# Sparse weights added float by float into a cleared DRAM array, and three blocks of tokens by rows instead of two

## The chip, the cores and the metric

One core of one Trainium2 chip runs the whole program. The metric is the device time in microseconds (us) of one execution. TensorE multiplies, VectorE (DVE), ScalarE (ACT) and GpSimd (POOL) work beside it, SyncE (SP) issues most DMAs, and all DMAs share 16 DMA engines.

## The reference, cut to what matters

One layer over 1024 tokens of width 1024: a mixing part (RG-LRU, SSD, a merge), which the change hardly touches, and then a layer of 16384 experts:

```
q = (x @ w_q)                       # 8 heads, two halves of 128
s = einsum(q, sub_keys)             # 128 scores per head and half
sv, si = top_k(s, 16)               # of each half
cv, ci = top_k(all 256 sums, 16)    # 16 experts per token and head
idx = i1 * 128 + i2;  g = softmax(cv)
act = gelu(sum_d expert_down[idx] * x)
y = sum over 8*16 experts of g * act * expert_up[idx]
```

Each token so uses 128 of the 16384 experts. Everything is float32; a product is made of three float32r products of the high and low parts.

## The kernel before, in words

The 1024 tokens are 8 blocks of 128. `NA = 2` blocks are computed **by rows**: for each of a token's 128 experts one indirect DMA of GpSimd fetches a row of `expert_down` for all 128 tokens (512 KB), and VectorE multiplies it with the tokens and sums (`dots`, L2002). The other 768 tokens (`TD`) are computed **dense**: TensorE multiplies all 128 tiles of 128 experts with them, and the result is later multiplied by a sparse array of weights that is zero for experts not chosen.

The stages that matter, each closed by a barrier of all engines:

- `project_in` (to about 850 us): 64 tiles of the input projection. SP loads a tile of weights, GpSimd cuts it into high and low part, TensorE multiplies.
- `queries` (1605 to 1872 us): 16 query tiles. TensorE makes queries (`query`, L1606, the first half as 256 + 256 columns, since the row tokens lie in a buffer of their own) and scores (`scores`, L1617). The scores of all blocks go to DRAM. VectorE chooses the experts of block 0, one head after each pair of tiles (`choose`: `select_keys`, then `select_picks`, whose end waits for an exponential of ScalarE).
- `experts_down` (1872 to 3384 us): 64 steps of two tiles of 128 experts. Per tile TensorE turns it (8 transposes, `turn`, L1864), ScalarE and VectorE cut it (`cut`, `low`, L1979), and TensorE makes 48 products of 128x384 (`products`, L1874); ScalarE applies the gelu and stores it in DRAM. Beside that each step chooses the experts of one head of one later block (56 of 64 steps), does four row products (`ROWS = 4` buffers), and from block 2 on builds the weights of 16 tokens: VectorE makes one-hot matrices (`hits`, L1988, L1992), TensorE multiplies them token by token (`weights`, L1885, 16 products a step), ScalarE copies them out (L1943), and SP stores them in DRAM as pieces of 64 tokens. `ps_d` and `downT` have one and two buffers.
- `experts_up` (3384 to 4649 us): 32 groups of four tiles. SP loads tile, gelu and weights (the weights in runs of 64 floats); VectorE multiplies the two; ScalarE, VectorE and GpSimd cut them (L2212, L2214, L2268, L2178); TensorE makes 12 slots of 12 products of 128x512 (`L2381`), which VectorE adds into `y_acc`. Beside that a group does two **quads** (L2340): four row fetches of GpSimd each (L2171), for four experts at once of 32 tokens each, and 8 products against `row_spread` (L2257). There is one set of row buffers.

The order of work on each engine is written out by hand; most of it stands in hardware loops (`Fori`) before. Every wait is on a semaphore, and each engine works in order, so what is written behind a waiting instruction waits too.

Of the kernel before, what the change touches and what calls it, by code (L numbers as in the profile page):

```python
# [40 lines left out]
NEG = -30000.0  # L41

# [315 lines left out]
def project_in(m, inp, keep, scratch):  # L358
# [10 lines left out]
    with ExitStack() as st:  # L369
# [6 lines left out]
        dt_bias = m.sb(st, "dt_bias", [P, SH])  # L376
        pre = m.sb(st, "conv_in", [P, 2, CW - 1 + T])
# [8 lines left out]
        s_abs, s_e, s_u, s_c = (m.sb(st, n, [P, NS]) for n in ("sp_abs", "sp_exp", "sp_one_plus", "sp_corr"))  # L386
# [16 lines left out]
        h_stored = m.sem("lru_h_stored")  # L403

# [18 lines left out]
        with nc.Block() as block:  # L423
            @block.sync
            def _(sp):
# [18 lines left out]
                for lo, hi, col in SEGMENTS[1:]:  # L444
                    pairs(sp, lo, hi, load(col))

            @block.gpsimd
# [944 lines left out]
SEL_STEPS = 25  # L1392

SCORES_READ = 6

def selection(m, st, tag):
# [3 lines left out]
    for name, shape, dt in (("scores", [P, 2, PK], F32), ("scores_rest", [P, 2, PK], F32), ("top", [P, 2, TOPK], F32),  # L1402
# [3 lines left out]
                            ("ij_f", [P, 2, TOPK], F32), ("neg_max", [P, 1], F32),  # L1406
                            ("exp", [P, TOPK], F32), ("exp_sum", [P, 1], F32), ("inv", [P, 1], F32)):
        b[name] = m.sb(st, f"{tag}_{name}", shape, dt)
    b["hit"] = m.sb(st, f"{tag}_hit", [P, 2, TOPK, TOPK])
# [3 lines left out]
def select_keys(dve, b, step, keep, n):  # L1413

    sc, rest, top, idx = b["scores"], b["scores_rest"], b["top"], b["idx"]

    def after(k):
        dve.wait_ge(step, (n + 1) * SEL_STEPS + k)

    after(0)
    alone(dve, keep["dve_passed"])
# [3 lines left out]
    alone(dve, keep["dve_passed"])  # L1426
# [4 lines left out]
    alone(dve, keep["dve_passed"])  # L1431
# [3 lines left out]
    alone(dve, keep["dve_passed"])  # L1435
# [6 lines left out]
def select_picks(dve, b, step, exp_done, keep, n, out):  # L1442
# [3 lines left out]
    iota, idx = keep["iota_row"], b["idx"]  # L1446

    def after(k):
        dve.wait_ge(step, (n + 1) * SEL_STEPS + k)
# [3 lines left out]
    alone(dve, keep["dve_passed"])  # L1453
# [3 lines left out]
    alone(dve, keep["dve_passed"])  # L1457
# [4 lines left out]
    alone(dve, keep["dve_passed"])  # L1462
    dve.max(b["cv"][:, 8:16], flat(b["cand_rest"])).then_inc(step, 1)
    after(17)
    alone(dve, keep["dve_passed"])
# [14 lines left out]
    dve.reduce_sum(out(slice(1, 3)), b["hit"][:], axis=AX.X).then_inc(step, 1)  # L1480
    dve.wait_ge(exp_done, n + 1)
# [994 lines left out]
```

## Time and profile before

| | us |
|---|---|
| three runs | 4647.34, 4653.0, 4651.68 (median 4651.68) |
| the profiled execution | 4650.75 |
| its span, first to last instruction | 4649.0 |
| PE busy in it | 4286.5 (92%) |
| DVE busy | 2599.5 (56%) |
| ACT busy | 1341.0 (29%) |
| POOL busy | 1432.2 (31%) |
| HBM read and written | 674.03 MB and 163.58 MB |

PE is TensorE's products, PEld its weight loads, which overlap them. Shares of busy time are means over the stages. Matmuls are pipelined: a row's duration is longer than the distance to the next one, and it is the distance that adds up to time.

### The profile page before, as it was taken

What the parts mean: (1) busy time and instruction counts of PE and PEld (TensorE: products, weight loads), DVE (VectorE), ACT (ScalarE), POOL (GpSimd) and SP (SyncE); (2) the same over time, 40 slices, a digit from 0 to 9 for tenths busy, and PEclk for the clock granted to TensorE, in tenths of its full rate; (3) what the DMA queues carried; (4) which work ended last, traced back from release to release, by engine and by line L of the source; (5) the groups of instructions that cost most, each with busy time, mean ns of one, the idle gap of its engine ahead of it and who ended that gap; (6) DMA issues with size and microseconds to landing.
All of it is one profiled execution on the core that took longest, in us unless ns stands there. A gap on an engine that the chain in (4) does not pass through costs nothing. (4 is left out here: it accounts for less than half of the span.)

```text
span 4649.0 us, 69126 instructions
## 1 busy us (share of the span) xinstructions
PE 4286.5 (92%) x22902; PEld 3639.0 (78%) x22933; DVE 2599.5 (56%) x5422; ACT 1341.0 (29%) x2021; POOL 1432.2 (31%) x1022
## 2 busy tenths in 40 slices
PE   8999999897997799799999999999979999999998
PEld 3788877686776689798999999999957777777776
DVE  3555211255665333677889898897644444444444
ACT  1132433344222421233333333333221111111112
POOL 0333333354334021222111111111144444444442
PEclk9999999899998899899999999999989999999999
DMA  7222233344562422555566665666587777777776
GB/s 272 56 95 95 99 104 98 93 118 118 165 195 90 152 64 63 177 198 197 173 215 218 204 207 198 219 215 210 199 270 245 248 246 249 246 250 248 251 248 213
DMA packets 632585, 838.99 MB, mean 180 GB/s; under 512 B 227732, under 2 KB 448164, under 8 KB 632484
## 3 DMA queue, kind: packets, MB, share of 16 engines
q1 hardware_dynamic: 514468, 476.96, 32.5%
q0 software_dynamic: 73728, 268.47, 17.3%
q10 hardware_dynamic: 44288, 92.29, 5.1%
q8 instruction: 54, 0.88, 0.1%
q14 instruction: 47, 0.39, 0.0%
HBM read 674.03 MB, written 163.58 MB: 180 GB/s over the span
## 5 line engine op out<-in xcount | busy, mean ns | idle before, releaser
L1874 PE MATMUL p_u<-h2T_hi,downT_hi 128*128 128x384 f32 x2048 | 715.0, 349 | 103.4 <-DVE downT_lo L1979 85.3
L1874 PE MATMUL p_u<-h2T_hi,downT_lo 128*128 128x384 f32 x2048 | 693.9, 339 | 0.0
L1874 PE MATMUL p_u<-h2T_lo,downT_hi 128*128 128x384 f32 x2048 | 692.8, 338 | 0.0
L1852 POOL DMA_INDIRECT down_rows<-in_peer_down_dram,row_ids x256 | 262.4, 1025 | 1264.4 <-DVE row_dots L2002 1187.8
L2381 PE MATMUL p_y<-up_hi,coef_hi 128*128 128x512 f32 x1488 | 587.2, 395 | 0.0
L2381 PE MATMUL p_y<-up_lo,coef_hi 128*128 128x512 f32 x1488 | 580.4, 390 | 0.0
L2381 PE MATMUL p_y<-up_hi,coef_lo 128*128 128x512 f32 x1488 | 579.4, 389 | 0.0
L2282 DVE TENSOR_TENSOR y_acc<-p_y,y_acc 128x512 f32<-128x512 f32 x372 | 256.4, 690 | 540.5 <-PE p_y L2381 540.5
L1874 PEld LDWEIGHTS p_u<-h2T_hi,downT_hi 128*128 128x128 f32 x2048 | 391.3, 191 | 116.4 <-issue 116.4
L2178 POOL TENSOR_TENSOR up_lo<-up_raw,up_hi 128x1024 fp32r<-128x1024 f32 x128 | 323.0, 2524 | 419.8 <-ACT up_hi L2212 418.7
L508 PE MATMUL p<-hT_hi,w_hi 128*128 128x512 f32 x1024 | 405.0, 396 | 0.0
L508 PE MATMUL p<-hT_hi,w_lo 128*128 128x512 f32 x1024 | 398.8, 389 | 0.0
L508 PE MATMUL p<-hT_lo,w_hi 128*128 128x512 f32 x1024 | 398.6, 389 | 0.0
L1874 PEld LDWEIGHTS p_u<-h2T_lo,downT_hi 128*128 128x128 f32 x2048 | 391.7, 191 | 0.0
L1874 PEld LDWEIGHTS p_u<-h2T_hi,downT_lo 128*128 128x128 f32 x2048 | 390.5, 191 | 0.0
L2381 PEld LDWEIGHTS p_y<-up_hi,coef_hi 128*128 128x128 f32 x1488 | 279.5, 188 | 111.3 <-issue 54.5
L2214 ACT CAST coef_hi<-gelu_in 128x768 fp32r<-128x768 f32 x128 | 106.8, 834 | 793.8 <-DVE gelu_in L2266 793.8
L2171 POOL DMA_INDIRECT up_rows<-in_peer_up_dram,row_ids_turned x256 | 263.4, 1029 | 226.3 <-PE p_rows L2340 161.8
L2381 PEld LDWEIGHTS p_y<-up_hi,coef_lo 128*128 128x128 f32 x1488 | 279.5, 188 | 59.4
L2381 PEld LDWEIGHTS p_y<-up_lo,coef_hi 128*128 128x128 f32 x1488 | 279.6, 188 | 56.2
L2002 DVE CUSTOM_DVE_ANT_0 row_products<-down_rows,x_tok_rows 128x1024 f32<-128x1024 f32 x256 | 311.8, 1218 | 12.1 <-DVE row_u L2010 6.4
L1931 ACT ACTIVATE gelu_out<-p_u 128x384 f32<-128x384 f32 x256 | 126.6, 495 | 595.3 <-PE p_u L1874 594.5
(343 smaller groups left out, 7888.8 us busy)
## 6 DMA issues: line engine op xcount, KB each, us to landing
down_raw<-in_peer_down_dram SPq DMA_DIRECT2D x128, 512.0 KB, 4.4
up_raw<-in_peer_up_dram SPq DMA_DIRECT2D x128, 512.0 KB, 5.3
scratch_gu<-gelu_out ACTq DMA_DIRECT2D x128, 384.0 KB, 2.3
gelu_in<-scratch_gu SPq DMA_DIRECT2D x128, 384.0 KB, 4.1
weights_in<-scratch_w SPq DMA_DIRECT2D x128, 384.0 KB, 6.4
w_raw<-in_w_in_dram SPq DMA_DIRECT2D x64, 512.0 KB, 4.0
w_ada_sb<-in_w_ada_dram SPq DMA_DIRECT2D x12, 2048.0 KB, 15.4
scratch_w<-weights_out SPq DMA_DIRECT2D x48, 512.0 KB, 3.7
```

The lines of the kernel that those rows point to most:

```text
L508: mm = pe.matmul(ps[u][:, half, :], w[:, u, k, :], hT[h][:, k, half * TH:(half + 1) * TH], start=(n == 0), stop=(n == 3 * KD - 1))
L1852: pool.indirect_dma_start(out=rows[:, n % ROWS, :], out_offset=None, in_=inp["peer_down"][0], in_offset=bass.IndirectOffsetOnAxis(ap=row_i ...
L1874: mm = pe.matmul(ps_u[u][half][:, 0:HD], d[:, u, k, :], h2[h][:, k, half * HD:(half + 1) * HD], start=(n == 0), stop=(n == 3 * KD - 1))
L1931: act.activation(gu[:, u, half * HD:(half + 1) * HD], ps_u[u][half][:, 0:HD], ACT.Gelu).then_inc(gelu_done[u][half], 1)
L2002: dve.tensor_tensor_reduce(junk[:], rows[:, j, :], x_tok[:, a], 1.0, 0.0, ALU.mult, ALU.add, dot[:, j:j + 1]).then_inc(dot_done, 1)
L2171: pool.indirect_dma_start(out=rows[:, j, :], out_offset=None, in_=inp["peer_up"][0], in_offset=bass.IndirectOffsetOnAxis(ap=ids_t[:, a, t: ...
L2178: pool.tensor_tensor(up_lo[:, g % 2, j, :], up_raw[:, u], up_hi[:, g % 2, j, :].bitcast(F32), ALU.subtract).then_inc(up_lo_done, 1)
L2214: act.copy(g_hi[:, v, j, :], gu[:, u]).then_inc(g_hi_done, 1)
L2282: dve.tensor_tensor(part, ps_y[s % BANKS][:], part, ALU.add).then_inc(added, 1)
L2381: mm = pe.matmul(ps_y[s % BANKS][:], a[:, v, j, t * P:(t + 1) * P], b[:, v, j, half * TH:(half + 1) * TH], start=(n == 0), stop=(n == 3 * ...
```

## The change

`NA` goes from 2 to 3: 384 tokens by rows, 640 dense (`TD = 640`, products of 320 columns, 10 slots instead of 12 in the up stage, three quads a group instead of two). The weights are no longer built with one-hot products. A DRAM array `w` of [128, 128, 640] floats is cleared in `project_in` by 64 stores of zeros, one behind each weight load on SP's queue. For each head of a dense block, 16 indirect DMAs of GpSimd, each of 128 single floats, one per token, add the weights into it (`send_weights`): 5 heads of block 3 in `queries`, 35 heads in `experts_down`. Before the first 16 of a head GpSimd waits for the previous head's 16 to have landed. In `queries` VectorE chooses 13 heads instead of 8.

```
-NA = 2
+NA = 3
@@ project_in, SP
                         sp.dma_start(w_raw[:, u], w_in(col, i)).then_inc(w_loaded[u], 16)
+                        if isinstance(i, int) and i == 0:
+                            sp.wait_ge(zero_set, 1)
+                        sp.dma_start(scratch["w"][bass.ds(i * CLEAR, CLEAR)].rearrange("e p t -> p e t"),
+                                     zero[:].unsqueeze(1).to_broadcast([P, CLEAR, TD])).then_inc(w_cleared, 16)
+                pool.memset(zero[:], 0.0).then_inc(zero_set, 1)
@@ new: the end of a head's choice, and the sending
+def select_end(dve, b, step, exp_done, n, id_f, ids, scale, weight, chosen):
+    dve.wait_ge(step, n * SEL_STEPS + 24)
+    dve.scalar_tensor_tensor(id_f, b["pick"][:, 0], float(PK), b["pick"][:, 1], ALU.mult, ALU.add).then_inc(step, 1)
+    dve.wait_ge(exp_done, n + 1)
+    dve.reciprocal(b["inv"][:], b["exp_sum"][:]).then_inc(step, 1)
+    dve.wait_ge(step, n * SEL_STEPS + 25)
+    if scale is None:
+        dve.tensor_copy(ids, id_f).then_inc(step, 1)
+    else:
+        dve.tensor_scalar(ids, id_f, float(TD), scale, ALU.mult, ALU.add).then_inc(step, 1)
+    dve.wait_ge(step, n * SEL_STEPS + 26)
+    dve.tensor_scalar(weight, b["exp"][:], b["inv"][:], None, ALU.mult).then_inc(chosen, 1)
+def send_weights(pool, b, w_flat, sent, chosen, k, part):
+    r, half = k % SENT, TOPK // 2
+    if part == 0:
+        pool.wait_ge(chosen, k + 1)
+        if k:
+            pool.wait_ge(sent[(k - 1) % SENT], 16 * TOPK * ((k - 1) // SENT + 1))
+    for j in range(part * half, part * half + half):
+        pool.indirect_dma_start(out=w_flat, out_offset=bass.IndirectOffsetOnAxis(ap=b["sent_ids"][:, r, j:j + 1], axis=0),
+                                in_=b["sent_g"][:, r, j:j + 1], in_offset=None, compute_op=ALU.add
+                                ).then_inc(sent[r], 16)
@@ queries, GpSimd, behind the cut of query tile n
+                    if n >= 5 and (n - 5) // 2 < EARLY:
+                        send_weights(pool, sel, w_flat, sent, weights_chosen, (n - 5) // 2, (n - 5) % 2)
@@ experts_down, order of heads: 16 pairs (dense, fetched), then 19 dense, over steps 0 to 59
+        fetched = [(a, h) for a in range(1, NA) for h in range(PH)]
+        dense = [(NA, h) for h in range(EARLY, PH)] + [(b, h) for b in range(NA + 1, TB) for h in range(PH)]
+        heads = [x for pair in zip(dense, fetched) for x in pair] + dense[len(fetched):]
@@ experts_down, GpSimd: 6 fetches a step (RING = 14 buffers), and the head of two steps before
+                for c in range(2 * FETCH):
+                    fetch(c)
+                for s in range(STEPS + 2):
+                    for c in range((s + 2) * FETCH, min((s + 3) * FETCH, TA)):
+                        fetch(c)
+                    if s >= 2 and head_of(s - 2) is not None and heads[head_of(s - 2)] in dense:
+                        for part in range(2):
+                            send_weights(pool, sel, w_flat, sent, weights_chosen, k, part)
+                        k += 1
@@ experts_down, VectorE: one step
+                    if 2 * s + 2 < E1:
+                        low(2 * s + 2)
+                    if before is not None:
+                        choose(before)
+                    for c in range(s * FETCH, s * FETCH + FETCH // 2):
+                        dot(c)
+                    if head is not None:
+                        dve.wait_ge(s_loaded[head % 2], 16 * (head // 2 + 1))
+                        select_keys(dve, sel, step, head)
+                    if 2 * s + 3 < E1:
+                        low(2 * s + 3)
+                    for c in range(s * FETCH + FETCH // 2, (s + 1) * FETCH):
+                        dot(c)
+                    if head is not None:
+                        select_picks(dve, sel, step, iota, head)
-                def hits(hh, r, ws, b):
-                def weights(ws, pair):
-                def keep_weights(hh, r, ws, b):
-                def store_piece(tile, hh, piece, stored=None):
@@ experts_up: two sets of row buffers, three quads a group
+    SETS = 2 if NA > 2 else 1
+    SPREADS = 2 * NA
+                        sp.dma_start(w[:, u], scratch["w"][n]).then_inc(w_loaded[u], 16)
+                        for q in range(NA):
+                            if s == (q + 1) * SLOTS // (NA + 1):
+                                quad(g * NA + q)
```

Further: `raw`, `downT` and the gelu buffer get four buffers and `ps_d` two; the weights' low cut and the choices are ordered anew as shown; the loops of `queries` and `experts_up`, and those of `experts_down` but for TensorE's, are written out instead of looped; a row product writes its sum straight to its place (`keep_dots` and its copy go); the query tile's first half is 384 + 128 columns; a third block of tokens is turned in `queries`.

## Rows read from the trace of the kernel before

**Rows 1.** Windows: busy us (instructions) by engine, granted clock, DMA share, GB/s.

```profile
110.00:850.00 740.00, 728.84 (x3138) 584.71 (x3137) 246.05 (x173) 227.71 (x217) 246.14 (x148) 0.99 0.28 90
1605.00:1872.00 267.00, 236.61 (x1568) 219.31 (x1568) 98.77 (x314) 58.09 (x91) 57.53 (x34) 0.92 0.27 83
1872.00:3384.00 1512.00, 1389.46 (x8722) 1371.07 (x8722) 1244.37 (x3684) 520.99 (x804) 262.44 (x256) 0.98 0.61 204
3384.00:3446.00 62.00, 41.88 (x180) 29.36 (x180) 34.71 (x37) 17.49 (x20) 32.28 (x18) 0.83 0.96 305
3446.00:4636.00 1190.00, 1146.53 (x5457) 862.39 (x5454) 536.80 (x685) 227.47 (x261) 554.23 (x367) 1.00 0.74 244
```

**Rows 2.** The longest wait of TensorE: us in total, times, longest.

```profile
PE p_u L1874 <- DVE downT_lo L1979: 85.3, 51, 2.8
```

**Rows 3.** Timeline of TensorE in the down stage: start us, us, instruction.

```profile
1912.15 0.33 PE L1874 MATMUL p_u<-h2T_hi,downT_hi 128*128 128x384 f32 x1
...
1918.74 0.34 PE L1874 MATMUL p_u<-h2T_hi,downT_lo 128*128 128x384 f32 x1
...
1919.71 0.42 PE L1874 MATMUL p_u<-h2T_hi,downT_hi 128*128 128x384 f32 x1
```

**Rows 4.** Timeline of TensorE in the up stage, 65 products apart, then a quad.

```profile
3501.42 0.39 PE L2381 MATMUL p_y<-up_hi,coef_lo 128*128 128x512 f32 x1
3501.74 1.92 PE L2340 MATMUL p_rows<-up_rows,row_spread 128*32 128x512 f32 x16
3503.59 0.50 PE L2381 MATMUL p_y<-up_hi,coef_hi 128*128 128x512 f32 x1
...
3505.10 0.39 PE L2381 MATMUL p_y<-up_hi,coef_hi 128*128 128x512 f32 x1
...
3519.86 0.39 PE L2381 MATMUL p_y<-up_hi,coef_lo 128*128 128x512 f32 x1
```

**Rows 5.** Timeline of TensorE in the queries: 128 columns, then 256.

```profile
1779.83 0.27 PE L1617 MATMUL p_s<-keys_lo,q_hi 128*128 x1
...
1781.95 0.28 PE L1617 MATMUL p_s<-keys_hi,q_lo 128*128 x1
...
1782.96 0.28 PE L1606 MATMUL p_q<-h2T_hi,wq_hi 128*128 128x256 f32 x1
...
1787.76 0.28 PE L1606 MATMUL p_q<-h2T_hi,wq_lo 128*128 128x256 f32 x1
```

**Rows 6.** Timeline of VectorE: first and last instruction of one head's choice.

```profile
1861.65 0.49 DVE L1424 MAX8 query_sel_top<-query_sel_scores 128x8 f32<-128x128 f32 x2 [6.83 <-ACT query_sel_scores L1655]
...
1870.74 0.23 DVE L1484 TENSOR_SCALAR chosen<-query_sel_exp,query_sel_inv 128x16 f32<-128x16 f32 x1
```

**Rows 7.** Timeline of VectorE, down stage: a difference, a row product, its read-out.

```profile
2634.37 1.22 DVE L1979 TENSOR_TENSOR downT_lo<-p_down,downT_hi 128x1024 fp32r<-128x1024 f32 x1
2635.51 1.22 DVE L2002 CUSTOM_DVE_ANT_0 row_products<-down_rows,x_tok_rows 128x1024 f32<-128x1024 f32 x1
2636.64 0.08 DVE L2002 DVE_READ_ACCUMULATOR2_ANT row_dots<- 128x1 f32 x1
```

**Rows 8.** Timeline of GpSimd, up stage: row fetches back to back.

```profile
3565.90 0.94 POOL L2171 DMA_INDIRECT up_rows<-in_peer_up_dram,row_ids_turned  x1 [0.31 <-issue]
3567.14 0.94 POOL L2171 DMA_INDIRECT up_rows<-in_peer_up_dram,row_ids_turned  x1 [0.30 <-issue]
```

**Rows 9.** The row fetches of GpSimd: group of the page, then durations min/median/max.

```profile
L1852 POOL DMA_INDIRECT down_rows<-in_peer_down_dram,row_ids x256 | 262.4, 1025 | 1264.4 <-DVE row_dots L2002 1187.8
...
L1852 POOL DMA_INDIRECT down_rows<-in_peer_down_dram,row_ids x256: 932/937/1803, 1881.3 to 3351.3; - x128
```

**Rows 10.** DMA queues of the page: packets, MB, share of 16 engines.

```profile
q1 hardware_dynamic: 514468, 476.96, 32.5%
q0 software_dynamic: 73728, 268.47, 17.3%
q10 hardware_dynamic: 44288, 92.29, 5.1%
```

More of the change, by code:

```diff
@@ L41 @@
 NEG = -30000.0
+NA = 3
+TA = NA * P
+TD = T - TA
+ND = TB - NA
+HD = TD // 2
+E1 = 128
 VEC = {}
@@ L1757, in experts_down, with row @@
+        def row(c):
+            r = c % RING
+            return keep["y_acc"][:, r, :] if r < TB else more_rows[:, r - TB, :]
+        loaded = [m.sem(f"down_loaded{i}") for i in range(4)]
+        s_loaded = [m.sem(f"scores_loaded{i}") for i in range(2)]
+        turned = m.sem("down_turned")
         hi_done, lo_done = m.sem("down_hi_done"), m.sem("down_lo_done")
@@ L1771, in experts_down @@
+        rows_loaded = [m.sem(f"down_rows_loaded{i}") for i in range(RING)]
+        dot_done = m.sem("row_dot_done")
         down = inp["peer_down"][0].rearrange("(e p) d -> e p d", p=P)
-        PE1 = E1 // PIECES
-        def steps(eng, o, w, last, step_of):
-            half = STEPS // 2
-            at = None if w is None else w * STEPS
-            for hh in range(2):
-                end = last and hh == 1
-                with eng.Fori(0, half - end) as r:
-                    step_of(hh, r, o * STEPS + hh * half + r, None if w is None else at + hh * half + r, True)
-            if last:
-                step_of(1, half - 1, TB * STEPS - 1, ND * STEPS - 1, False)
@@ L1840, in _, with load, load_scores @@
-                for hh in range(2):
-                    sp.wait_ge(w_stored[hh], 16 * (PIECES * (ND - hh) + 1))
-                    sp.wait_ge(gu_stored[hh], 16 * (E1 // 2 + 1))
+                def load(n):
+                    if n >= 4:
+                        sp.wait_ge(turned, n - 3)
+                    sp.dma_start(raw[:, n % 4], down[n]).then_inc(loaded[n % 4], 16)
+                def load_scores(n):
+                    b, h = heads[n]
+                    if n >= 2:
+                        sp.wait_ge(step, (n - 2) * SEL_STEPS + SCORES_READ)
+                    sp.dma_start(sel["scores"][:, n % 2], scratch["scores"][b * PH + h]).then_inc(s_loaded[n % 2], 16)
@@ L1844, in _ @@
+                load(0)
+                load(1)
+                load(2)
+                load(3)
+                for s in range(STEPS):
+                    for n in (2 * s + 4, 2 * s + 5):
+                        if n < E1:
+                            load(n)
+                    if s + 1 < STEPS and head_of(s + 1) is not None:
+                        load_scores(head_of(s + 1))
+                for r in range(4):
+                    sp.wait_ge(gu_stored[r], 16 * (E1 // 4))
             @block.gpsimd
@@ new lines, in store @@
+                def store(n):
+                    for half in range(2):
+                        act.wait_ge(gelu_done[n % 2][half], n // 2 + 2)
+                    act.dma_start(scratch["gu"][n], gu[:, n % 4]).then_inc(gu_stored[n % 4], 16)
+                cut(0)
+                cut(1)
+                for n in range(E1):
+                    gelu(n, 0)
+                    if n + 2 < E1:
+                        cut(n + 2)
+                    if n % 2 == 0 and n and head_of(n // 2 - 1) is not None:
+                        select_act(act, sel, step, exp_done, head_of(n // 2 - 1))
+                    gelu(n, 1)
+                    store(n)
@@ new lines, in _ @@
+                low(0)
+                low(1)
+                for s in range(STEPS):
+                    head, before = head_of(s), None if s == 0 else head_of(s - 1)
+                    if 2 * s + 2 < E1:
[13 more added lines that the diff above has]
+                        select_picks(dve, sel, step, iota, head)
@@ L2214, in cut @@
                         act.copy(g_hi[:, v, j, :], gu[:, u]).then_inc(g_hi_done, 1)
-                groups(act, cut)
+                        if j == 1:
+                            for a in range(NA - 1):
+                                if (QUADS * (a + 1) - 1) // NA + 1 == g:
+                                    keep_rows(a)
                 act.wait_ge(eps_set, 1)
@@ L2385, in group @@
                         mm.then_inc(y_mm, 1)
-                        if isinstance(g, int) and g == GROUPS - 1 and s == SLOTS - 4:
-                            quad(2 * GROUPS - 1, 1)
-                groups(pe, group)
 def build(nc, inp, out):
```

734 lines of the change are left out of this document (288 added, 446 removed).

## Prediction

> **What bounds the kernel now.** I read the windows of the stages first, then TensorE's waits, then the timelines for distances between instructions. TensorE's products are back to back nearly everywhere: 1389 of 1512 us in the down stage and 1147 of 1190 in the steady up stage, at a granted clock of 0.98 to 1.00, that is 2.4 GHz [rows 1]. Its longest wait is 85 us for VectorE's `downT_lo` [rows 2], so in the down stage VectorE (1244 of 1512 us busy) is a near second. What counts is the distance of the products. 38 of them with 384 columns lie in 6.59 us, 0.173 each [rows 3]; 65 with 512 in 14.76, 0.227 [rows 4]; 40 with 256 in 4.80, 0.120, and 19 with 128 in 2.12, 0.112 [rows 5]. From 256 up that is a straight line (0.054 per 128 columns), so 320 columns will take 0.147; at 128 something else, 0.112, is the floor. A tile's eight transposes add 0.97 - 0.17 = 0.80 [rows 3], a quad 2.17 - 0.23 = 1.94 [rows 4]. DMA is at 0.61 in the down stage and 0.74 in the up stage [rows 1].
>
> **Input projection.** The clears are 64 stores of 655 KB, 42 MB, one behind each weight load on SP's queue. The stage moves 90 GB/s at a DMA share of 0.28 [rows 1]; 42 MB over 740 us add 57 GB/s. A load is issued two tiles (about 22 us) ahead, and a clear in front of it is some 2 us of the engines. Hidden; SP's one new wait and GpSimd's memset, ahead of its first cut, cost about 1 us. If the cover were gone, 64 times 2 us would be 128, which the share excludes.
>
> **Queries, 267 us now.** The first half's pair of 256 columns becomes 384 + 128: 24 pairs in 16 tiles, each 0.173 + 0.112 - 0.240 = 0.045 more, 17 us. Turning and copying a third block costs about 4 (bounds 0 and 6). A tile then takes 24 x (0.173 + 0.112) + 24 x 0.227 + 24 x 0.112 = 15.0 us. VectorE chooses one more head in five of the pairs of tiles: a head is 9.3 us [rows 6], 9.9 with its two new small instructions, so 2 x 9.9 + 2 x 1.14 = 22 of 30 us. GpSimd gets eight sends behind each of ten cuts; the next cut, and so TensorE's next tile, is queued behind them and behind the waits for `chosen` and for the last head's landing. Its own work is 57.5 us over 16 tiles, 3.6 each [rows 1]; with sends of 1.33 us (below) 14.2 of 15.0. It fits, barely. Sum +21.
>
> **Down stage, 1512 us now.** TensorE loses the one-hot products and a sixth of the columns: a tile is 48 x 0.147 + 0.80 = 7.85 us, a step 15.7, 64 steps 1005. It is no longer the bound. VectorE loses `hits` and gets two more row products a step: 6 row products and 2 differences at 1.14 [rows 7] and 9.9 for a head make 19.0, with waits 19.1 us in the 51 steps with a head; otherwise TensorE's 15.7 stands. GpSimd has 384 fetches (12 ahead of the steps) and 35 x 16 = 560 sends. A fetch takes 1.025 us in the mean [rows 9] and the next starts 0.30 behind its end (1.24 apart at 0.94 each) [rows 8], so 1.33. No row shows a send. Below, it cannot beat the shortest fetch by much, since it too names 128 addresses: 0.93 + 0.30; above, I take the longest fetch, 1.80 + 0.30 = 2.10 [rows 9]. I take 1.33, the nearest row being the fetch.
>
> The sends of a step are queued ahead of the next step's fetches, but 14 buffers hold over two steps of rows, so VectorE and GpSimd run apart by that much and only their sums count. Steps 0 to 37 hold 32 heads, every second one dense: VectorE 32 x 19.1 + 6 x 15.7 = 705 us; GpSimd about 240 x 1.33 + 256 x 1.33 = 660, hidden. From there on all 19 heads are dense: GpSimd has 144 fetches and 304 sends left, 448 x 1.33 = 596 us, against VectorE's 19 x 19.1 + 7 x 15.7 = 473. GpSimd is the bound, and VectorE waits for rows. With 20 us for the start, the last landing and the barrier: 705 + 596 + 20 = 1321, that is -191. The lower bound, sends that VectorE hides, is 1198 (-314).
>
> The deeper buffers (four of `downT`, two of `ps_d`) and the exponential moved a step back take away the 85 us of [rows 2]; they count nothing extra, since TensorE no longer sets the pace.
>
> The DMA engines: a fetch is 0.173 x 4649 / 512 = 1.57 us of all 16 [rows 10]; 384 of them 603, the tiles (67 MB at queue 1's 316 GB/s) 212, gelus (42 MB at queue 10's 389 GB/s) 108, scores 21: 944 us without the floats. These are 560 x 128 / 16 = 4480 per engine. Queue 1's mean packet takes 0.047 us, queue 0's 4096-byte ones 0.196 [rows 10]; between them 211 and 878 us. I take the lower, by size: 1155 us, below 1321.
>
> **Up stage, 1265 us now.** A group has 120 products and three quads: 27.2 + 5.8 = 33.1 us, now 1190 / 31 = 38.4 [rows 1] for 32.7 + 3.9 + waits. I add 1 us for rows that land late. GpSimd is busy 554 / 31 = 17.9 us a group [rows 1], 8 fetches at 1.03 and 9.7 of cuts; now 12 x 1.33 + 9.7 = 26, hidden; its fetches wait for quads, with the next cuts behind them, but the second row set lets each be issued a quad earlier. The first group is 62 - 24 x 0.227 + 2 x 1.94 = 60.5, the end 13 as now: 60.5 + 31 x 34.1 + 13 = 1131, -135 (without waits 1099, -165). The weights are read as rows of 2560 bytes instead of 256, which relieves the engines, while rows grow: 11.0 MB a group instead of 9.4, at 34.1 us 323 GB/s. Queue 0 alone would do 334 [rows 10]. That is close.
>
> **The sum**, against the profiled execution's own 4650.75 (its span 4649.0; 0.02% under the median 4651.68): +1 + 21 - 191 - 135 = -304, so 4347 us.
>
> **Rival 1, the floats crowd the DMA engines (slower).** Each float is a read, an addition and a write in DRAM, on the ring that also carries the row fetches. At 0.196 us each the engines have 944 + 878 + 20 = 1842 us of work in the down stage (+330), and the whole is 4868. It decides from (1625 - 964) / 4480 = 0.148 us per float; 1625 is the down stage at which the whole comes out even. For it: the trace has nothing of the kind, and the waits for landing forbid overlap of heads. Against: small packets are cheap in queue 1. The Trainium skill (DMA: Bandwidth & Descriptors, Latency and other measured facts) gives HBM access as 0.2 us in the mean; if each float waited for one such read alone, its estimate would be 4480 x 0.2 = 896 us, this rival. No run here shows it yet.
>
> **Rival 2, a send costs GpSimd more than a fetch.** At 2.10: 384 x 1.33 + 560 x 2.10 + 20 = 1707 us in the down stage (+195), and in the queries eight sends and a cut are 20.4 us in a 15.0 us tile, 54 over ten: 4787. Even at 1.89. For it: adding may need another descriptor per float; against: as many addresses as a fetch.
>
> **Rival 3, DMA bounds the up stage.** At the 305 GB/s of the start of that stage, where the share is 0.96 [rows 1], a group takes 36.1 us: 60.5 + 1119 + 13 = 1193 (-72), the whole 4410.
>
> **Chances.** Forecast 0.57, own range 4250 to 4430; rival 3 0.12; rival 2 0.11, of it 0.04 still faster; rival 1 0.20. Faster by over 0.2% (what a measurement of this kernel tells from no change) 0.57 + 0.12 + 0.04 = 0.73, within 0.02, slower 0.25. The low end is both lower bounds, 4651 - 314 - 165 + 17 = 4189, rounded to 4200. The high end, 4720, takes in most of rival 2 and the mildest of rival 1; about 0.2 is left out.
>
> **What would show it.** Products of 320 columns 0.147 apart; in the down stage VectorE without gaps in the first 700 us, then row products waiting for `down_rows` while GpSimd is never idle; sends about 1.3 us apart; a down stage near 1320. In the up stage groups of 34 us with `p_rows` hardly waiting for `up_rows`. Wrong, if GpSimd waits for its own sends to land (rival 1), if sends are 2 us apart (rival 2), or if `up_rows` end TensorE's waits (rival 3).

## The result: 1.8% slower, 4734.56 us instead of 4651.18

Four runs of the changed kernel gave 4732.07 to 4734.94 us (median 4734.56), four of the kernel before beside them 4647.34 to 4653.0 (median 4651.18): a ratio of 1.0179, 95% interval 1.0162 to 1.0197. The forecast was 4347 with a range of 4200 to 4720, so it was wrong in sign and by 388 us. Rival 2 (a send costs GpSimd more than a fetch, 4787) is what happened.

By stages, from the first instruction of one to the first of the next, in the profiled executions (spans 4649.0 and 4732.6):

| stage | before | after | difference | forecast |
|---|---|---|---|---|
| up to the queries | 1604.8 | 1603.8 | -1.0 | +1 |
| queries | 267.6 | 318.6 | +51.0 | +21 |
| down | 1512.5 | 1700.4 | +187.9 | -191 |
| up | 1264.0 | 1109.8 | -154.2 | -135 |

Windows of the kernel after (us, busy us and instructions of PE, PEld, DVE, ACT, POOL, granted clock, DMA share, GB/s), the counterpart of [rows 1]:

```profile
110.00:850.00 740.00, 728.05 (x3138) 584.64 (x3137) 245.21 (x172) 227.55 (x216) 246.95 (x149) 0.99 0.45 146
1604.00:1922.00 318.00, 269.62 (x1576) 249.32 (x1576) 143.00 (x515) 53.92 (x106) 181.35 (x115) 0.89 0.33 66
1922.00:2600.00 678.00, 533.81 (x3584) 526.05 (x3585) 500.29 (x1388) 194.76 (x295) 535.02 (x373) 0.90 0.76 238
2600.00:3300.00 700.00, 429.99 (x2762) 422.64 (x2760) 398.43 (x1103) 153.36 (x232) 579.33 (x397) 0.80 0.64 172
3300.00:3624.00 324.00, 132.93 (x827) 130.23 (x827) 118.30 (x296) 40.21 (x64) 260.17 (x177) 0.70 0.49 113
3690.00:4720.00 1030.00, 1030.00 (x5158) 722.59 (x5157) 560.19 (x649) 218.46 (x262) 679.40 (x482) 1.00 0.90 326
```

In the up stage TensorE is busy 1030.00 of 1030 us. In the down stage no engine looks full: TensorE falls from 534 of 678 us to 133 of 324, VectorE likewise. GpSimd, with 535 of 678, 579 of 700 and 260 of 324, is the busiest, and its 947 instructions have 0.30 us between them that do not count as busy: 1374 + 947 x 0.30 = 1658 of the 1702 us. It is full. DMA, at 0.76, 0.64 and 0.49, is not.

The groups of GpSimd's DMAs (busy us, mean ns, idle before), the counterpart of [rows 9]. `scratch_w` is the array `w`; eight of the 14 row buffers lie in `y_acc`, so the fetches stand in two groups:

```profile
L1525 POOL DMA_INDIRECT scratch_w<-down_sel_sent_g,down_sel_sent_ids x560 | 947.3, 1692 | 170.7 <-issue 167.0 <-DVE row_u L1969 3.7
L1525 POOL DMA_INDIRECT scratch_w<-query_sel_sent_g,query_sel_sent_ids x80 | 126.5, 1581 | 35.2 <-issue 22.8 <-DVE query_sel_sent_g L1513 12.4
L1870 POOL DMA_INDIRECT y_acc<-in_peer_down_dram,row_ids x222 | 250.0, 1126 | 125.0 <-issue 100.2 <-DVE row_u L1969 20.8 <-DMA scratch_w<-down_sel_sent_g,down_sel_sent_ids 4.0
L1870 POOL DMA_INDIRECT down_rows<-in_peer_down_dram,row_ids x162 | 177.1, 1093 | 58.2 <-issue 44.8 <-DVE row_u L1969 10.1 <-DMA scratch_w<-down_sel_sent_g,down_sel_sent_ids 3.4
```

Durations min/median/max, first and last start:

```profile
L1525 POOL DMA_INDIRECT scratch_w<-down_sel_sent_g,down_sel_sent_ids x560: 1548/1556/2672, 2003.9 to 3611.8; - x187
L1525 POOL DMA_INDIRECT scratch_w<-query_sel_sent_g,query_sel_sent_ids x80: 1548/1557/2061, 1701.0 to 1880.1; - x80
```

A send takes 1.556 us in the median and 1.692 in the mean, where the forecast had a fetch's 1.025, and (947.3 + 170.7) / 560 = 2.00 us with the idle time ahead of it. The fetches' mean rose from 1.025 to (250.0 + 177.1) / 384 = 1.11, so 1.41 apart. The last send starts at 3611.8, and the up stage starts 11 us later. The longest waits of the down stage (us in total, times, longest), beside [rows 2]:

```profile
PE p_u L1907 <- DVE downT_lo L1960: 429.1, 43, 22.9
DVE row_products L1969 <- DMA y_acc<-in_peer_down_dram,row_ids: 351.5, 48, 30.0
DVE row_products L1969 <- DMA down_rows<-in_peer_down_dram,row_ids: 195.5, 48, 27.3
POOL scratch_w L1525 <- issue: 167.0, 548, 0.3
```

This is the chain: VectorE waits 547 us for fetched rows, and with it stands the next tile's low part, for which TensorE waits 429 us. GpSimd itself waits 42 us for others in the whole stage (the last parts of its groups above); the rest of its idle time in the stage is its own 0.30 us. The DMA queues of the page, beside [rows 10]:

```profile
q1 hardware_dynamic: 337108, 451.14, 29.5%
q0 software_dynamic: 202752, 403.07, 28.4%
q10 hardware_dynamic: 42240, 82.85, 4.6%
```

### The profile page after: what moved, and what is told of

Same layout as the page of the kernel before. It is cut to its first block and busy times, and to the rows that moved or that the text cites. A ratio compares the mean times of both kernels' runs of the same rounds, so it can differ in the third digit from the quotient of the medians.

```text
span 4732.6 us, 59021 instructions
## 1 busy us (share of the span) xinstructions
PE 3911.7 (83%) x21133; PEld 3237.4 (68%) x21133; DVE 2446.7 (52%) x4690; ACT 1195.0 (25%) x1822; POOL 2808.5 (59%) x1921
## 3 DMA queue, kind: packets, MB, share of 16 engines
q0 software_dynamic: 202752, 403.07, 28.4%
## 5 line engine op out<-in xcount | busy, mean ns | idle before, releaser
L1907 PE MATMUL p_u<-h2T_hi,downT_hi 128*128 128x320 f32 x2048 | 681.5, 333 | 531.2 <-DVE downT_lo L1960 429.1
L1525 POOL DMA_INDIRECT scratch_w<-down_sel_sent_g,down_sel_sent_ids x560 | 947.3, 1692 | 170.7 <-issue 167.0
L1907 PE MATMUL p_u<-h2T_lo,downT_hi 128*128 128x320 f32 x2048 | 660.1, 322 | 0.0
L1907 PE MATMUL p_u<-h2T_hi,downT_lo 128*128 128x320 f32 x2048 | 658.3, 321 | 0.7 <-issue 0.7
L2098 POOL DMA_INDIRECT up_rows<-in_peer_up_dram,row_ids_turned x384 | 419.0, 1091 | 239.3 <-PE p_rows L2261 144.2
L2300 PE MATMUL p_y<-up_lo,coef_hi 128*128 128x512 f32 x1240 | 485.5, 392 | 0.0
L2300 PE MATMUL p_y<-up_hi,coef_lo 128*128 128x512 f32 x1240 | 482.7, 389 | 0.0
L1969 DVE CUSTOM_DVE_ANT_0 row_products<-y_acc,x_tok_rows 128x1024 f32<-128x1024 f32 x222 | 264.0, 1221 | 351.8 <-DMA y_acc<-in_peer_down_dram,row_ids 351.5
L1870 POOL DMA_INDIRECT y_acc<-in_peer_down_dram,row_ids x222 | 250.0, 1126 | 125.0 <-issue 100.2
L1969 DVE CUSTOM_DVE_ANT_0 row_products<-down_rows,x_tok_rows 128x1024 f32<-128x1024 f32 x162 | 193.7, 1222 | 196.1 <-DMA down_rows<-in_peer_down_dram,row_ids 195.5
```

Source lines behind the costliest of these rows:

```text
L1525: pool.indirect_dma_start(out=w_flat, out_offset=bass.IndirectOffsetOnAxis(ap=b["sent_ids"][:, r, j:j + 1], axis=0), in_=b["sent_g"][:, r, ...
L1870: pool.indirect_dma_start(out=row(c), out_offset=None, in_=inp["peer_down"][0], in_offset=bass.IndirectOffsetOnAxis(ap=row_ids[:, a, k:k + ...
L1907: mm = pe.matmul(ps_u[u][half][:, 0:HD], d[:, i, k, :], h2[h][:, k, half * HD:(half + 1) * HD], start=(n == 0), stop=(n == 3 * KD - 1))
L1969: dve.tensor_tensor_reduce(junk[:, c % 2], row(c), x_tok[:, a], 1.0, 0.0, ALU.mult, ALU.add, row_u[:, a, k:k + 1]).then_inc(dot_done, 1)
L2098: pool.indirect_dma_start(out=rows[:, n % SETS, j, :], out_offset=None, in_=inp["peer_up"][0], in_offset=bass.IndirectOffsetOnAxis(ap=ids_ ...
L2300: mm = pe.matmul(ps_y[s % BANKS][:], a[:, v, j, t * P:(t + 1) * P], b[:, v, j, half * TH:(half + 1) * TH], start=(n == 0), stop=(n == 3 * ...
```

## The experiments

Theory A says that GpSimd's time for sends and fetches sets the down stage. Its rivals: something else in the new stage (rows that land late, the order, the clock), or the DMA engines. Stages as in the table above, of one profiled execution each; "sends" are those of the down stage. The times of the first row and of the last two are medians of four runs, the others are single runs; the runs of one kernel lie within 0.5% of each other.

| kernel | fetches, sends | queries | down | up | time |
|---|---|---|---|---|---|
| after | 384, 560 | 318.6 | 1700.4 | 1109.8 | 4734.56 |
| no sends | 384, 0 | 317.8 | 1053.8 | 1110.6 | 4088.37 |
| half the sends | 384, 280 | 315.3 | 1198.9 | 1110.2 | 4231.32 |
| plain sends | 384, 560 | 284.4 | 1433.2 | 1110.2 | 4432.89 |
| no query sends | 384, 560 | 284.6 | 1706.9 | 1110.1 | 4708.88 |
| NA = 2 | 256, 688 | 312.0 | 1735.3 | 1219.5 | 4873.01 |
| NA = 4 | 512, 432 | 314.7 | 1661.4 | 1120.8 | 4701.76 |
| half-height sends | 384, 560 | 305.4 | 1637.6 | 1109.8 | 4658.34 |
| no row products | 384, 560 | 318.7 | 1600.0 | 1109.9 | 4634.15 |
| adding fetches | 384, 560 | 315.1 | 1919.9 | 1109.8 | 4950.31 |
| sums, plain sends | 384, 560 | 290.2 | 1466.5 | 1109.6 | 4469.64 |
| sums, NA = 4 | 512, 432 | 281.1 | 1460.7 | 1112.3 | 4469.55 |

### Without the sends of the down stage

```
-                        for part in range(2):
-                            send_weights(pool, sel, w_flat, sent, weights_chosen, k, part)
+                        pool.wait_ge(weights_chosen, k + 1)
```

The waits for their landing go too.

> The changed kernel with all 560 sends of experts_down left out (the weights of 35 heads are not added). Theory A, GpSimd's sends set the pace of the down stage: the stage falls from 1700 us to the VectorE bound, about 1200 to 1250 us, and the whole kernel to 4235 to 4290 us. Rival B, the stage is slow for another reason (waits for rows that land late, TensorE's lower granted clock, the written-out order): the stage stays above 1500 us, the kernel above 4530 us. Rival C, the accumulated floats crowd the DMA engines: the stage falls too, but then the row fetches' DMA time falls with it and the half kernel tells the two apart.

Measured: 4088.37 us, the stage 1053.8. Its window:

```profile
1922.00:2976.00 1054.00, 1024.56 (x7168) 1015.73 (x7168) 1001.28 (x2783) 389.82 (x589) 444.20 (x384) 0.99 0.86 301
```

VectorE is busy 1001 of 1054 us and TensorE 1025, at a clock of 0.99, with DMA at 0.86. So the sends cost 647 us, and with the same rows and the same order the stage is far below the 1500 of B, which falls. The packets of 4 KB of the fetches take 0.189 us in the mean in this stage's trace, and 0.178 with all the sends, so the floats do not slow the rows. The stage is even shorter than my lower bound of 1198.

### Half of the sends

```
-    r, half = k % SENT, TOPK // 2
+    r, half = k % SENT, count // 2        # count = 8 in the down stage
```

> The changed kernel with 8 instead of 16 sends for each head of experts_down (half of the weights are not added). Theory A at 2.0 us a send and 1.4 us a fetch: in the first 38 steps GpSimd needs 12 x 1.4 + 8 x 2.0 = 33 us a pair of steps, less than VectorE's 38; in the later 22 it needs 22 us a step against VectorE's 19; the stage takes about 1280 us, the kernel about 4315 us. If the price of a send were that of a fetch and the time lay elsewhere, half of the sends would take away half of what all of them take (kernel near 4485 us).

Measured: 4231.32 us, the stage 1198.9 (expected 1280 with VectorE's old price). The two windows:

```profile
1920.00:2560.00 640.00, 621.68 (x4360) 616.41 (x4361) 608.50 (x1704) 239.03 (x358) 506.63 (x351) 0.99 0.88 306
2560.00:3119.00 559.00, 428.78 (x2811) 421.68 (x2809) 401.23 (x1080) 150.08 (x231) 455.86 (x314) 0.89 0.74 218
```

The first 280 sends cost 145 us, the other 280 cost 501, or 1.79 us each: as A says, most of the first 280 run beside VectorE. In the first window VectorE is busy 609 of 640 us; in the second GpSimd has 456 + 314 x 0.30 = 550 of 559, with half the floats and DMA at 0.74, so it is GpSimd and not the engines (rival C) that is full.

### Sends that overwrite instead of adding

```
-                                in_=b["sent_g"][:, r, j:j + 1], in_offset=None, compute_op=ALU.add
+                                in_=b["sent_g"][:, r, j:j + 1], in_offset=None
```

> The changed kernel with every send as a plain scatter that overwrites instead of adding (experts that two heads of a token chose lose one of the two weights). Theory D, the addition is what makes a send cost GpSimd 1.55 us against 0.94 for a fetch: the send falls to about 0.94 us, its distance to 1.24, the stage to about 1300 us and the kernel to about 4330 us. Theory E, it is the scattered write of 128 single floats: the send stays at 1.55 us and the kernel within 20 us of 4735.

Measured: 4432.89 us. The group of the sends:

```profile
L1525 POOL DMA_INDIRECT scratch_w<-down_sel_sent_g,down_sel_sent_ids x560 | 662.8, 1184 | 170.7 <-issue 161.3 <-DVE row_u L1969 9.1 <-DVE down_sel_sent_g L1513 0.3
```

Durations min/median/max:

```profile
L1525 POOL DMA_INDIRECT scratch_w<-down_sel_sent_g,down_sel_sent_ids x560: 965/972/2057, 1967.1 to 3309.9; - x187
```

The median fell from 1.556 to 0.972 us, near a fetch's 0.937 [rows 9]. So D holds: the addition costs GpSimd 0.58 us a send (and not by full DMA engines: in the query stage of the changed kernel, at a DMA share of 0.33, an added send's median is the same 1.557), and a scattered write of single floats costs what a fetch of rows does. The stage took 1433 us rather than the expected 1300, since the means stay above the medians (1.18 for a send, 1.16 for a fetch).

### Without the sends of the query stage

```
-                    if n >= 5 and (n - 5) // 2 < EARLY:
-                        send_weights(pool, sel, w_flat, sent, weights_chosen, (n - 5) // 2, (n - 5) % 2)
+                pool.wait_ge(weights_chosen, EARLY)
```

Here too the waits for landing go.

> The changed kernel with the 80 sends of the query stage left out (the weights of 5 heads are not added). Theory A, the cuts of the query weights queue behind the sends on GpSimd: the stage falls from 318 us to about 288, the kernel to about 4705 us. Rival F, VectorE's 13 choices set the stage: it stays at 310 to 318 us and the kernel within 10 us of 4735.

Measured: 4708.88 us, the stage 284.6. So 34 of the 51 us are GpSimd's cuts behind the sends, and 17 the rest (forecast 21). With plain sends the stage takes 284.4: at 0.97 us a send they fit beside TensorE, at 1.56 they do not. The kernel gains only 26 us, as its down stage took 6.5 us longer, which was not looked into.

### The sending alone, with two blocks by rows

```
-NA = 3
+NA = 2
```

> The changed kernel with NA = 2: 256 tokens by rows, the weights of 768 tokens sent (688 sends in experts_down), so the sending and the new order alone, without the third block. Theory A, GpSimd's time of the down stage is 1.49 us a fetch and 2.0 us a send (what the changed kernel shows for 384 and 560 of them: 572 + 1118 of 1700 us): 256 x 1.49 + 688 x 2.0 = 1757, the stage about 1767 us, the up stage near that of before (1264), the kernel about 4950 us. Rival G, the third block of row fetches is what overloads GpSimd: with 128 fetches fewer the kernel is below 4735.

Measured: 4873.01 us, the down stage 1735.3 (expected 1767), the up stage 1219.5. G is refuted: with 128 fetches fewer and 128 sends more the kernel is 138 us slower. So the change's two halves pull apart: against before, the sending, with the new order and buffers that come with it, is +222 us, and the third block on top of it -138. The up stage gains 45 us of its 154 with two blocks still, from what else the change does there (weights read in rows instead of 64-float runs, the order written out); which of these was not tried.

### Four blocks by rows

```
-NA = 3
+NA = 4
@@ queries, TensorE
-                        parts = ((h2a, 0, 0, TA), (h2, 0, TA, TH)) if half == 0 else ((h2, TH - TA, 0, TH),)
+                        parts = ((h2a, 0, 0, TA),) if half == 0 else ((h2, TH - TA, 0, TH),)
-RING = 14
+RING = 16
@@ experts_up, GpSimd: fetch(n + 1) behind cut(g, 1), fetch(n + 2) behind cut(g, 2)
```

> The changed kernel with NA = 4: 512 tokens by rows, 512 dense, 432 sends in experts_down, row ring of 16. Theory A: 512 x 1.49 + 432 x 2.0 = 1627, the down stage about 1637 us; the up stage by TensorE 8 slots x 12 x 0.227 x 32 + 128 quads x 1.94 = 945 us, or by GpSimd 512 x 1.38 + cuts 306 = 1013, so 970 to 1050; the kernel 4530 to 4610 us, faster than both. Rival G (row fetches are the load): slower than 4735.

Measured: 4701.76 us. The down stage took 1661.4 (expected 1637), but the up stage 1120.8 rather than 970 to 1050. Its window:

```profile
3620.00:4690.00 1070.00, 974.44 (x5032) 621.72 (x5028) 624.63 (x636) 211.86 (x271) 790.15 (x623) 0.97 0.96 371
```

TensorE's longest wait there:

```profile
PE p_rows L2261 <- DMA up_rows<-in_peer_up_dram,row_ids_turned: 70.1, 47, 5.0
```

The DMA share is 0.96 at 371 GB/s, and TensorE waits for rows to land. So it is rival 3 of the prediction, a DMA-bound up stage, one block later; with three blocks the stage ran at 0.90 and 326 GB/s without a wait. GpSimd is not far behind, with 790 + 623 x 0.30 = 977 of the 1070 us, and no run takes the load off one of the two alone. Over 256, 384 and 512 fetches the down stage takes 1735, 1700 and 1661 us: 128 fetches in place of 128 sends save 35 to 39 us, not the 76 of 128 x (2.00 - 1.41), as a fetch's mean rises from (149.2 + 113.1) / 256 = 1.02 us to (307.4 + 302.2) / 512 = 1.19 (the run without row products, below, shows why).

### Sends of 64 partitions

```
-...ap=b["sent_ids"][:, r, j:j + 1]...  in_=b["sent_g"][:, r, j:j + 1]
+...ap=b["sent_ids"][0:P // 2, r, j:j + 1]...  in_=b["sent_g"][0:P // 2, r, j:j + 1]
```

> The changed kernel with every send of 64 partitions instead of 128 (the weights of half of each block's tokens are not added). Theory H, GpSimd writes a descriptor (or two, for an added float) for each token: the send falls from 1.55 to about 0.8 us, the down stage to about 1250 us, the kernel to about 4280. Theory I, the cost is one of the instruction: the send stays at 1.55 and the kernel within 20 us of 4735.

Measured: 4658.34 us; min/median/max of a send:

```profile
L1525 POOL DMA_INDIRECT scratch_w<-down_sel_sent_g,down_sel_sent_ids x560: 1392/1401/2509, 1990.4 to 3536.1; - x187
```

1.401 instead of 1.556 us: if the price is a straight line through the two, 2.4 ns a partition, 0.31 for 128, and 1.25 us that do not depend on their number. Neither theory held in full, but I is the nearer. Even if all of the 0.31 were the addition's, 0.27 of its 0.58 would be no price per token.

### Without the row products

```
-                    dve.tensor_tensor_reduce(junk[:, c % 2], row(c), x_tok[:, a], 1.0, 0.0, ALU.mult, ALU.add,
-                                             row_u[:, a, k:k + 1]).then_inc(dot_done, 1)
+                    dve.tensor_copy(row_u[:, a, k:k + 1], row(c)[:, 0:1]).then_inc(dot_done, 1)
```

> The changed kernel with VectorE's 384 row products left out (one element of the fetched row is copied in its place; all fetches and sends stay). Theory J, the two-input products of VectorE lengthen GpSimd's indirect DMAs: the mean send falls from 1.69 to its median of 1.55 us, the mean fetch from 1.11 to 0.94, the down stage to 560 x 1.86 + 384 x 1.24 = 1518 us, the kernel to about 4550. Theory K, the long ones have another cause: means and time within 30 us of before the edit (4735).

Measured: 4634.15 us, the stage 1600.0 rather than 1518; GpSimd's groups:

```profile
L1525 POOL DMA_INDIRECT scratch_w<-down_sel_sent_g,down_sel_sent_ids x560 | 879.2, 1570 | 170.7 <-issue 167.1 <-DVE row_u L1969 3.7
L1870 POOL DMA_INDIRECT y_acc<-in_peer_down_dram,row_ids x222 | 212.7, 958 | 135.9 <-issue 100.2 <-DVE row_u L1969 32.6 <-DMA scratch_w<-down_sel_sent_g,down_sel_sent_ids 3.0
L1870 POOL DMA_INDIRECT down_rows<-in_peer_down_dram,row_ids x162 | 154.8, 956 | 74.6 <-issue 44.8 <-DVE row_u L1969 27.7 <-DMA scratch_w<-down_sel_sent_g,down_sel_sent_ids 2.1
```

The means fell to 1.570 and 0.957 us, close to the medians of the changed kernel, so J holds for the durations: VectorE's two-input row products lengthen GpSimd's DMAs by 0.12 us a send and 0.155 a fetch in the mean, 128 us together. The stage gave 100 of them; my 1518 had left out GpSimd's waits for buffers (60 us). Two timelines of the changed kernel (start us, us) show how, GpSimd's first:

```profile
2743.33 0.94 POOL L1870 DMA_INDIRECT down_rows<-in_peer_down_dram,row_ids  x1 [0.30 <-issue]
2744.57 1.92 POOL L1870 DMA_INDIRECT down_rows<-in_peer_down_dram,row_ids  x1 [0.30 <-issue]
2746.80 2.67 POOL L1525 DMA_INDIRECT scratch_w<-down_sel_sent_g,down_sel_sent_ids  x1 [0.30 <-issue]
2749.77 1.58 POOL L1525 DMA_INDIRECT scratch_w<-down_sel_sent_g,down_sel_sent_ids  x1 [0.30 <-issue]
```

VectorE beside it:

```profile
2744.46 1.22 DVE L1969 CUSTOM_DVE_ANT_0 row_products<-down_rows,x_tok_rows 128x1024 f32<-128x1024 f32 x1
2745.60 1.23 DVE L1969 CUSTOM_DVE_ANT_0 row_products<-down_rows,x_tok_rows 128x1024 f32<-128x1024 f32 x1
2746.75 1.23 DVE L1969 CUSTOM_DVE_ANT_0 row_products<-y_acc,x_tok_rows 128x1024 f32<-128x1024 f32 x1
2747.89 0.49 DVE L1440 MAX8 down_sel_top<-down_sel_scores 128x8 f32<-128x128 f32 x2
```

The fetch and the send that start while products run take 0.98 and 1.11 us longer than their medians, about one product; the send beside `MAX8` and its like, which have one input, takes 1.58. The whole stage shows the same when its DMAs are sorted by where a product stood: the 124 sends that start while a product runs take 2.16 us in the mean, the 49 into which a product starts 1.557, and the other 387 also 1.557; for fetches it is 1.396 (131), 0.942 (71) and 0.974 (182). What lengthens a DMA is a product under way when it starts. The products themselves are not held up:

```profile
L1969 DVE CUSTOM_DVE_ANT_0 row_products<-y_acc,x_tok_rows x222: 1210/1221/1294, 1945.3 to 3586.6; 128x1024 f32<-128x1024 f32 x111
L1969 DVE CUSTOM_DVE_ANT_0 row_products<-down_rows,x_tok_rows x162: 1212/1220/1298, 1959.6 to 3547.4; 128x1024 f32<-128x1024 f32 x162
```

The 289 products that start inside a DMA of GpSimd take 1.221 us in the mean, the other 95 1.222. The Trainium skill (SBUF — State Buffer, "SBUF: two separate sides") says that a VectorE instruction with two SBUF inputs and a GpSimd instruction that reads SBUF exclude each other, and that the one that starts second waits for the whole of the first. The trace agrees where GpSimd starts second, with the size of one such block; where VectorE does, it shows no block. Why the two directions differ no run here shows.

### Adding fetches

```
                                             in_offset=bass.IndirectOffsetOnAxis(ap=row_ids[:, a, k:k + 1], axis=0),
+                                            compute_op=ALU.add
```

> The changed kernel with the 384 row fetches of experts_down as adding fetches (rows of 4 KB are added into their buffers, which GpSimd clears once before, some 15 us), so that the row products are those of sums of rows. Theory M, the addition costs GpSimd about 0.6 us an instruction, whatever is moved: the mean fetch goes from 1.11 to about 1.7 us, the down stage from 1700 to about 1945, the kernel to about 4980. Theory N, only scattered single floats pay it: the fetch stays at 1.1 us and the kernel is at 4750.

Measured: 4950.31 us, the stage 1919.9. The groups of the fetches:

```profile
L1871 POOL DMA_INDIRECT y_acc<-in_peer_down_dram,row_ids x222 | 378.4, 1704 | 77.5 <-issue 63.5 <-DVE row_u L1974 13.4 <-DMA scratch_w<-down_sel_sent_g,down_sel_sent_ids 0.3
L1871 POOL DMA_INDIRECT down_rows<-in_peer_down_dram,row_ids x162 | 274.8, 1696 | 53.1 <-issue 47.6 <-DVE row_u L1974 5.2 <-DMA scratch_w<-down_sel_sent_g,down_sel_sent_ids 0.3
```

Durations min/median/max of one group:

```profile
L1871 POOL DMA_INDIRECT y_acc<-in_peer_down_dram,row_ids x222: 1539/1557/2628, 1931.6 to 3796.6; - x111
```

The median is 1.557 us, that of a send to 1 ns, for rows of 4 KB read into SBUF. Theory M holds: it is the addition that GpSimd pays, not the single floats, the scatter or DRAM as the destination. Nor is it the number of packets, which for a fetch is the same with and without the addition (queue 0 has 202752 in both kernels). The DMA engines were 0.82 busy in this stage and GpSimd, with 1607 + 946 x 0.30 = 1890 of 1908 us, full. Predicted +245, measured +216.

### A version that beats both: sums on VectorE, plain sends

What the addition does can be done ahead of the sends. A head's 16 experts differ, and a head is sent when the one before has landed; so if each head sends the sum over all earlier heads that chose the same expert, the last write is right.

```
+def sum_same(dve, b, past, summed, h, sent_g, chosen):
+    w = h * TOPK
+    ids, gs = (keep[:].rearrange("p h k -> p (h k)")[:, 0:w].unsqueeze(1).to_broadcast([P, TOPK, w]) for keep in past[0:2])
...
+    dve.tensor_tensor(same, mine.unsqueeze(2).to_broadcast([P, TOPK, w]), ids, ALU.is_equal).then_inc(summed, 1)
...
+    dve.tensor_tensor(same, same, gs, ALU.mult).then_inc(summed, 1)
...
+    dve.reduce_sum(b["extra"][:], same, axis=AX.X).then_inc(summed, 1)
...
+    dve.tensor_tensor(sent_g, b["extra"][:], past[1][:, h], ALU.add).then_inc(chosen, 1)
-                                in_=b["sent_g"][:, r, j:j + 1], in_offset=None, compute_op=ALU.add
+                                in_=b["sent_g"][:, r, j:j + 1], in_offset=None
```

> The whole computation, by plain sends: VectorE keeps the experts and weights of the block's earlier heads, compares the new head's 16 experts with them, and adds the weights of equal ones, so that the last write to a float holds the sum and nothing needs to be added in DRAM (a head's sends already wait until the previous head's have landed). By the run with plain sends and no sums: query stage 285, down stage about 1433 us, as GpSimd still sets it; VectorE's sums are three operations of 896 elements on average, about 1.15 us each, 35 times 3.9 = 137 us, on top of the 1001 us that it is busy in the run without sends, so 1140 of 1433 and hidden. The kernel 4430 to 4470 us, against 4651 before. Rival L: the sums come late in VectorE's order, so that the row products are held up and GpSimd's fetches with them: over 4520 us.

Measured: median 4469.64 us (4461.53 to 4471.45, four runs) against 4649.54, ratio 0.9607, 95% interval 0.9591 to 0.9623. The group of the sends, then the down stage from 2600 us on:

```profile
L1548 POOL DMA_INDIRECT scratch_w<-down_sel_sent_g,down_sel_sent_ids x560 | 685.4, 1224 | 170.7 <-issue 163.4 <-DVE row_u L1999 7.0 <-DVE down_sel_sent_g L1535 0.3
```

The window:

```profile
2600.00:3340.00 740.00, 484.06 (x3045) 475.39 (x3043) 509.27 (x1255) 163.84 (x251) 589.05 (x496) 0.82 0.53 182
```

At the upper end of what was expected, 37 us above the plain sends without sums: the stage is 33 us longer, of which the sends' mean, 1.224 instead of 1.184 us, makes 23, and the fetches with GpSimd's waits before them the rest. GpSimd still sets it (589 + 496 x 0.30 = 738 of 740 us).

The same with `NA = 4` and a ring of 15 rows (with the 16 of the other run with four blocks, an array of the sums needs 7168 bytes a partition of SBUF where 6012 are left):

> The kernel with sums on VectorE and plain sends, with NA = 4 (512 tokens by rows, ring of 15 rows). GpSimd in the down stage: 512 fetches and 432 plain sends at 1.5 us each, 1416 us, stage 1420 to 1450 against 1467 with three blocks. The up stage about 1118 us as in the run with four blocks and added sends, where the DMA engines were 0.96 busy, against 1110. Kernel 4440 to 4470 us, within 0.7% of three blocks (4470): what the down stage gains stays, and the up stage gives nothing. Rival: with added sends the up stage was slowed by something of that run alone, and it falls below 1050 us here, the kernel below 4400.

Measured: median 4469.55 us (4458.02 to 4477.95), ratio 0.9624, interval 0.9608 to 0.964, so the same as with three blocks. The down stage is 1460.7 rather than 1420 to 1450, the up stage 1112.3. GpSimd sets the down stage (1114 + 937 x 0.30 = 1395 of 1440 us), and the up stage runs at a DMA share of 0.96 again. Two blocks with sums were not tried.

## Why the prediction was wrong

**The step that failed is the price of a send**: "I take 1.33, the nearest row being the fetch". It measured 2.00: 0.97 as for a plain send, 0.58 for the addition, 0.14 from the median to the mean (0.12 of it by the row products) and 0.30 between instructions. The upper bound of 2.10 from the longest fetch held, and at that bound the prediction had 4787 (measured 4735) with +195 in the down stage (+188) and +54 in the queries (+51). That it came so near is luck: the 16 longest fetches before, of 1.80 us, are those that start while a row product runs, and a send is dear for another reason. What in the addition costs GpSimd 0.58 us stays open; one more descriptor per float, as rival 2 had it, is not the whole of it, since at least 0.27 does not grow with the number of floats. The phrase that gave it a low chance, "as many addresses as a fetch", is true and beside the point: the plain send has as many and costs 0.97.

**The first stretch** (steps 0 to 37) was to hide GpSimd's 660 us behind VectorE's 705. At 2.00 and 1.41 a pair of steps is 16 x 2.00 + 12 x 1.41 = 49 us of GpSimd against VectorE's 38; VectorE waited for rows from the start (busy 500 of the first 678 us), not only in the second stretch. In all 560 x 2.00 + 384 x 1.41 = 1661 and the 38 us of waits ahead of fetches make the 1700 us, where the forecast had 944 x 1.33 = 1256.

**VectorE's step was too dear.** The lower bound of 1198 fell at 1053.8 without sends. A head's choice was priced at 9.9 us from a timeline in the query stage, where VectorE is idle for 1.1 of the 9.3 us [rows 6]; in the down stage it is (1001 - 598) / 51 = 7.9 us, 102 less over 51 heads, where 598 is the time in which row products, read-outs or differences run. And the 13 steps without a head were put at TensorE's 15.7 us, where VectorE has 598 / 64 = 9.3 to do: 83 less. Dearer products and idle time take 41 of this back. This did not show in the result, since VectorE was not the bound.

**The fetch** was priced at 1.33 and took 1.41. The rule that was weighed there pointed the right way. The Trainium skill (GPSIMD Engine Reference, Specifications) says that GpSimd shares its SBUF interfaces with VectorE and contends with instructions that have two SBUF inputs; that GpSimd is the one that loses is not in it, but is what the trace shows. The prediction gave it 40 us, in the second stretch alone; without the row products GpSimd's DMAs are 128 us shorter.

**Queries.** +21 without the sends was right to 4 us (284.6 - 267.6 = 17). "It fits, barely" failed with the price: 8 sends of 1.58 + 0.30 and a cut of 3.6 are 18.6 us in a tile of 15.0; over ten tiles 36, measured 34.

**Up stage.** Right: -154 for -135. TensorE has no wait left from the second group on, so a group takes (1109.8 - 60.5 - 13) / 31 = 33.4 us, not 34.1; the microsecond for late rows was not needed with 326 GB/s.

**Rival 1 fell.** In the down stage's trace the packets of 4 bytes that belong to the 71680 floats take 3541 us of one engine, 0.049 us a float, against the 0.148 from which it would have decided. So the lower guess, 0.047, was right, and with it the DMA term: 1155 us forecast, 0.66 x 1700 = 1122 measured. Had the send kept a fetch's price, the plain kernel shows what was to be had: 4432.89, faster by 4.7%. The mechanism of the forecast would have been right in part and the size still 86 us off: the down stage is 112 us longer than forecast there, as sends and fetches take 1.18 and 1.16 us in the mean instead of 1.025, and GpSimd sets the pace in its first 712 us too (548 + 451 x 0.30 = 683 of them, against VectorE's 590).

## What to carry to other kernels

Here an indirect DMA was paid for by the engine that issues it, per instruction, before it was paid for in bytes (0.97 us for 512 bytes, 0.94 for 512 KB): count the instructions, put 0.30 us between them, and where no row shows the form, treat an option such as an addition as a price of its own and not as the nearest form's. If the issuing engine then sets the stage, an error of that price counts in full, 560 times here, and the case that it is dearer needs more than the 0.11 it was given. An addition in the DMA is worth replacing by a sum on an engine that has room: here 127 us more of a VectorE that had room (1139 us busy in the down stage against 1012 in the run with plain sends) removed 0.58 us from the median of 560 sends.

## What the runs showed of the hardware that was not expected

- An adding indirect DMA of GpSimd takes 1.556 us for 128 single floats into DRAM and 1.557 us for 128 rows of 4 KB into SBUF; without the addition 0.972 and 0.937. With 64 partitions an adding one takes 1.401.
- Queue 0 has 202752 packets in the changed kernel, 131072 with plain sends and 122112 without the down sends. A fetch of 128 rows is 144 of them ([rows 10]: 73728 / 512), so an adding send is (202752 - 110592) / 640 = 144, and a plain one 20480 / 640 = 32. By the sizes in the trace the 144 are all of 4 bytes, one a float and 16 more, and the 32 are 16 of 32 bytes, eight floats each, and 16 of 4. The single floats cost the engines little: 0.049 us each when added, 16 x 0.014 / 128 = 0.002 when not.
- An added 4 KB row costs the engines more than a plain one: the 49152 packets of the down stage's rows take 0.339 us in the mean when added and 0.178 when not, 0.161 more each; queue 0's share goes from 28.4% of 4732.6 us to 36.5% of 4948.6.
- A row product under way when GpSimd starts an indirect DMA lengthens the DMA (sends 2.16 us against 1.557); a DMA under way does not lengthen a product (1.221 us against 1.222).
- Granted clock: TensorE's fell to 0.90, 0.80 and 0.70 in the down stage of the changed kernel, where it waited more and more, so part of the time at 1.2 instead of 2.4 GHz, and was 0.99 in the same stage without sends. Here it costs next to nothing, as GpSimd sets the pace.
- At a DMA share of 0.96 the up stage with four blocks moved 371 GB/s, where 305 had been seen before at the same share [rows 1]. A DMA share says that the engines are full, not at which rate.
